# Gated linear attention in a fused decoder layer: two heads' queries side by side as one block-diagonal operand, dense keys and states

## The reference

```
log_a = log_sigmoid(a_lr @ w_a2 + b_a) / 16
bcum  = cumsum of log_a within a chunk
q_t, k_t = q / 8 * exp(bcum), k * exp(-bcum)
o_intra = where(tril, q_t @ k_t.T, 0) @ v
state   = exp(b_last) * state + (k * exp(b_last - bcum)).T @ v      # per head, 64 x 128
o_inter = q_t @ state before the chunk
o = rmsnorm(o_intra + o_inter) * silu(r)
```

## Time and profile before

| | |
|---|---|
| Median of 3 runs | 1683.11 us (1680.85 to 1890.51) |
| Profiled execution, its own time | 1687.72 us |
| Its span (slowest core) | 1686.6 us (cores: 1673.0 to 1686.6) |
| PE busy | 1628.0 us, 97%, 7859 matmuls |
| VectorE / ScalarE busy | 872.0 us / 730.4 us |
| Mean granted clock of TensorE | 0.992 of full speed on this core |
| DMA | 249.10 MB, mean 148 GB/s |

### The profile page before, as it was taken

The page is one execution under the profiler, slowest core; times in us unless marked ns, Lnnn a source line. Parts: engine busy times, 40 slices in busy tenths (PEclk is TensorE's granted clock), DMA queues, the critical chain, the costliest instruction groups (busy, mean ns, idle before and its releaser), DMA issues.

```text
span 1686.6 us, 24322 instructions; the slowest of 8 cores (1673.0 to 1686.6 us)
## 1 busy us (share of the span) xinstructions
PE 1628.0 (97%) x7859; PEld 753.9 (45%) x7859; DVE 872.0 (52%) x1490; ACT 730.4 (43%) x1182; POOL 120.6 (7%) x228
## 2 busy tenths in 40 slices
PE   6999999998999999999999999999999999999997
PEld 2445444434444444444444444454444444444443
DVE  6662442435765566654565644645645464433336
ACT  5213001046872256952477862268993221210114
POOL 0102011100000000000000000000000011001000
PEclk9999999999999999999999999999999999999999
DMA  9779999898566575555998774886464455623212
GB/s 212 106 114 124 139 125 110 129 148 208 104 146 157 151 154 111 111 130 167 252 207 181 159 192 151 256 220 154 133 192 129 159 157 157 178 70 100 76 38 100
DMA packets 80425, 249.10 MB, mean 148 GB/s; under 512 B 9440, under 2 KB 13808, under 8 KB 79856
## 3 DMA queue, kind: packets, MB, share of 16 engines
q0 software_dynamic: 28864, 107.49, 38.2%
q1 hardware_dynamic: 51440, 140.06, 26.9%
HBM read 282.91 MB, written 54.00 MB: 200 GB/s over the span
## 4 chain that ended last, share of the span: by engine, by line
PE 89%; DMA 4%; DVE 3%; ACT 3%; issue 2%; POOL 0%; DVEq 0%; ACTq 0%; SPq 0%; POOLq 0%
PE ps_all L562 88%; DMA ring<-f1g 2%; ACT mb L588 1%; DVE hS L600 1%; DMA ring<-wb 1%; ACT ma L588 1%; ACT L588 1%; DMA ring<-f2d 1%; DVE ntm L600 0%; DMA hS<-x 0%; DVE mb L595 0%; ACT fa L588 0%; DVE aF L595 0%; DVE gU L600 0%; ACT B L611 0%
## 5 line engine op out<-in xcount | busy, mean ns | idle before, releaser
L562 PE MATMUL ps_all<-ntm,ring 128*128 128x512 bf16 x2224 | 530.5, 381 | 5.1 <-ACT ma L588 2.2
L562 PE MATMUL ps_all<-B,ring 128*128 128x512 bf16 x2016 | 450.4, 379 | 2.8 <-DVE gU L600 1.0
L562 PEld LDWEIGHTS ps_all<-ntm,ring 128*128 128x128 bf16 x2224 | 216.3, 98 | 267.1 <-issue 21.1
L588 ACT ACTIVATE fa<-ps_all 128x512 f32<-128x512 f32 x170 | 101.4, 598 | 468.9 <-PE ps_all L562 460.5
L562 PEld LDWEIGHTS ps_all<-B,ring 128*128 128x128 bf16 x2016 | 195.9, 98 | 237.7 <-issue 8.3
L562 PE MATMUL ps_all<-aF,ring 128*128 128x512 bf16 (+1 forms) x1264 | 294.3, 375 | 3.7 <-DVE hS L600 1.7
L600 DVE SCALAR_TENSOR_TENSOR hS<-ps_all,hS 128x512 f32<-128x512 f32 (+1 forms) x256 | 170.0, 672 | 99.6 <-PE ps_all L562 98.4
L595 DVE TENSOR_TENSOR aF<-fa,ps_all 128x512 bf16<-128x512 f32 x148 | 101.3, 686 | 226.0 <-PE ps_all L562 219.6
L562 PEld LDWEIGHTS ps_all<-aF,ring 128*128 128x128 bf16 x1264 | 123.4, 98 | 147.5 <-issue 10.7
L588 ACT ACTIVATE mb<-ps_all 128x512 bf16<-128x512 f32 (+1 forms) x304 | 161.5, 576 | 39.0 <-PE ps_all L562 36.0
L588 ACT ACTIVATE ma<-ps_all,hv 128x512 f32<-128x512 f32 x104 | 71.2, 687 | 183.1 <-PE ps_all L562 162.2
(11 more groups left out here) (129 smaller groups left out, 1215.1 us busy)
## 6 DMA issues: line engine op xcount, KB each, us to landing
ring<-wb SPq DMA_DIRECT2D x112, 512.0 KB, 4.4
ring<-f1g POOLq DMA_DIRECT2D x44, 512.0 KB, 10.4
ring<-f2bg POOLq DMA_DIRECT2D x44, 512.0 KB, 3.6
wb<-wm POOLq DMA_DIRECT2D x28, 512.0 KB, 14.7
ma<-spill SPq DMA_DIRECT2D x48, 256.0 KB, 5.5
ring<-wb SPq DMA_DIRECT2D x48, 256.0 KB, 3.7
ring<-f2g POOLq DMA_DIRECT2D x22, 512.0 KB, 8.6
f2bg<-ring SPq DMA_DIRECT2D x22, 512.0 KB, 5.5
```

What stands on the lines that cost most here:

```text
L562: i = e.matmul(_ap(o), lhsT=_ap(l), rhs=_ap(r), start=st, stop=sp)
L588: f.add([("act", lambda e: e.activation(out=_ap(out), in_=_ap(in_), func=func, scale=_ap(scale), **kw), c_act(out, bias is not None))], ou ...
```

## The change

- q of a pair is written into `qz[pr]` (128 x 1024), block-diagonal: head 0's 64 rows in the columns 0 to 511, head 1's 64 rows in 512 to 1023, the rest zero. Two products on 64 rows in place of one on 128.
- k is used as it is. `ktz` and its copies are gone.
- The scores of a pair are one matmul of 256 columns with the moving operand [128, 2, 128] taken from qz.
- The state of a pair is dense, 128 rows (two heads' keys) by 128 value columns: `gU` and `gS` are 128x128. Block-diagonal q selects the head. `blk` and its load are gone. gU is updated in two pieces of 64 rows, from the two diagonal blocks of `pd`, and gS by a tensor_scalar.
- In the output, the carried product comes first, one matmul of 256 columns a pair, then v by am for each head, 128 columns.
- v's weights are cut in halves of K, all 512 columns: 8 matmuls of 512 columns for 128 tokens.
- k's working tile is kept until the last chunk; q needs none.

```
-    ktz = [T(f.sb(f"ktz{i}", [128, TT], BF16)[:], f"ktz{i}") for i in range(4)]
+    qz = [T(f.sb(f"qz{i}", [128, 2 * TT], BF16)[:], f"qz{i}") for i in range(2)]
-    gU = [T(f.sb(f"gU{i}", [128, 256], F32)[:], f"gU{i}") for i in range(2)]
+    gU = [T(f.sb(f"gU{i}", [128, 128], F32)[:], f"gU{i}") for i in range(2)]
...
-        f.dma("pool", blk, blk_d, nbytes=131072, after=f.last_pe)
...
 u_q:
-                stt(st["q"].bf()[:, pr * TT:(pr + 1) * TT], p, 0.125, st["E"][pr], ALU.mult, ALU.mult)
+                for o2 in range(2):
+                    rows = slice(64 * o2, 64 * o2 + 64)
+                    stt(qz[pr][rows, o2 * TT:(o2 + 1) * TT], p[rows, :], 0.125, st["E"][pr][rows, :], ALU.mult, ALU.mult)
 u_k:
-                for o2 in range(2):
-                    o = o2 * 64
-                    cp(ktz[pr * 2 + o2][o:o + 64, :], kb[o:o + 64, pr * TT:(pr + 1) * TT], eng="dve", rate=4.0)
 u_v:
-                st["wv"] = [mload("gv", i, 8) for i in range(2)]
+                st["wv"] = [mload("gv", i, 4) for i in range(2)]
...
-                mm([(p[:, v * 256:(v + 1) * 256], nM[k][:, i * 128:(i + 1) * 128], st["wv"][v][:, k, :], k == 0, k == 7)
-                    for v in range(2) for k in range(8)])
+                mm([(p, nM[k][:, i * 128:(i + 1) * 128], st["wv"][k // 4][:, k % 4, :], k == 0, k == 7) for k in range(8)])
 u_chunk:
-            q = [st["q"].bf()[:, pr * TT + i * 128:pr * TT + (i + 1) * 128] for pr in range(2)]
+            q = [qz[pr][:, :].re("p (h n) -> p h n", h=2)[:, :, csl] for pr in range(2)]
+            k = [st["k"].bf()[:, pr * TT + i * 128:pr * TT + (i + 1) * 128] for pr in range(2)]
...
-            mm([(pa[:, h4 * 128:(h4 + 1) * 128], ktz[h4][:, csl], q[h4 // 2], True, True) for h4 in range(4)])
+            mm([(pa[:, pr * 256:(pr + 1) * 256].re("p (h n) -> p h n", h=2), k[pr], q[pr], True, True) for pr in range(2)])
...
-            for h4 in range(4):
-                o = po[:, h4 * 128:(h4 + 1) * 128]
-                g.append((o, v[:, h4 * 128:(h4 + 1) * 128], am[:, h4 * 128:(h4 + 1) * 128], True, False))
-                g.append((o, gS[n % 2][h4 // 2][:, (h4 % 2) * 128:(h4 % 2 + 1) * 128], q[h4 // 2], False, True))
+            for pr in range(2):
+                g.append((po[:, pr * 256:(pr + 1) * 256].re("p (h n) -> p h n", h=2), gS[n % 2][pr], q[pr], True, False))
+                for h4 in (2 * pr, 2 * pr + 1):
+                    hsl = slice(h4 * 128, (h4 + 1) * 128)
+                    g.append((po[:, hsl], v[:, hsl], am[:, hsl], False, h4 % 2 == 1))
...
-                stt(gU[pr], gU[pr], gp, pd[:, pr * 256:(pr + 1) * 256], ALU.mult, ALU.add)
-                stt(gS[(n + 1) % 2][pr], gU[pr], gdec[par][pr][:, i:i + 1], blk, ALU.mult, ALU.mult)
+                for o2 in range(2):
+                    rows = slice(64 * o2, 64 * o2 + 64)
+                    stt(gU[pr][rows, :], gU[pr][rows, :], gp[rows, :],
+                        pd[rows, pr * 256 + o2 * 128:pr * 256 + (o2 + 1) * 128], ALU.mult, ALU.add)
+                ts(gS[(n + 1) % 2][pr], gU[pr], gdec[par][pr][:, i:i + 1], None, ALU.mult)
...
-    raw_at = [o_mla + [o_gla[:, i, :] for i in range(4)], o_x + ktz]
+    raw_at = [o_mla + [o_gla[:, i, :] for i in range(4)], o_x + [qz[i // 2][:, i % 2 * TT:(i % 2 + 1) * TT] for i in range(4)]]
```

More of the change, by code:

```diff
@@ L468, in build_program @@
     ident_d = din("ident", [128, 128])
-    blk_d = din("blk", [128, 256])
     smask_d = din("smask", [128, TT])
@@ L523, in build_program @@
     ident = T(f.sb("ident_s", [128, 128], BF16)[:], "ident")
-    blk = T(f.sb("blk_s", [128, 256], BF16)[:], "blk")
     smask = T(f.sb("smask_s", [128, TT], BF16)[:], "smask")
@@ L528, in build_program @@
     eps_c = T(f.sb("eps_c", [128, 1], F32)[:], "eps_c")
-    gU = [T(f.sb(f"gU{i}", [128, 256], F32)[:], f"gU{i}") for i in range(2)]
-    gS = [[T(f.sb(f"gS{j}_{i}", [128, 256], BF16)[:], f"gS{j}_{i}") for i in range(2)] for j in range(2)]
+    gU = [T(f.sb(f"gU{i}", [128, 128], F32)[:], f"gU{i}") for i in range(2)]
+    gS = [[T(f.sb(f"gS{j}_{i}", [128, 128], BF16)[:], f"gS{j}_{i}") for i in range(2)] for j in range(2)]
     gdec = [[T(f.sb(f"gd{j}_{i}", [128, 4], F32)[:], f"gd{j}_{i}") for i in range(2)] for j in range(2)]
@@ L678, in late_constants @@
             memset(gS[0][i], 0.0)
-        for i in range(4):
-            memset(ktz[i], 0.0)
+        for i in range(2):
+            memset(qz[i], 0.0)
         for kc in range(16):
@@ L984, in u_gates @@
                 st["Ei"].append(l)
-            st["q"], st["k"] = M2.get(), M2.get()
+            st["k"] = M2.get()
         def u_q():
@@ L1012, in u_kt @@
             cp(st["kt"].bf(), pb, rate=1.9)
-            M2.put(st["k"])
         def u_v(half):
             if half == 0:
-                st["wv"] = [mload("gv", i, 8) for i in range(2)]
+                st["wv"] = [mload("gv", i, 4) for i in range(2)]
                 st["v"] = [M2.get() for _ in range(2)]
@@ L1062, in u_chunk @@
             if i == 3:
-                M2.put(st["q"], st["kt"], *st["v"])
+                M2.put(st["k"], st["kt"], *st["v"])
         def u_x(hh):
@@ L1463, in _prep_shared @@
     for i in range(2):
-        block("gv", i, w_in[:, o[5] + i * 256:o[5] + (i + 1) * 256])
+        block("gv", i, w_in[i * 512:(i + 1) * 512, o[5]:o[6]])
         block("gr", i, w_in[:, o[7] + i * 256:o[7] + (i + 1) * 256])
@@ L1482, in _prep_shared @@
     f2g, f2d = ffn_w("ffn2_wg", "ffn2_wu", "ffn2_wd")
-    blk = np.zeros((128, 2, 128), f32)
-    blk[0:64, 0] = 1.0
-    blk[64:128, 1] = 1.0
     smask = np.ones((128, TT), f32)
@@ L1488, in _prep_shared @@
     return {
-        "vecs": vecs, "utri": (jj <= tq).astype(f32), "ident": (jj == tq).astype(f32), "blk": blk.reshape(128, 256),
+        "vecs": vecs, "utri": (jj <= tq).astype(f32), "ident": (jj == tq).astype(f32),
         "smask": smask, "wa2": np.ascontiguousarray(g("gla_w_a2")[0]),
```

## The result

After: 1692.02 us, median of 7 runs (1688.95 to 1976.87). Before, on the same chip: 1681.70 us, median of 7 (1680.25 to 1890.51). The ratio is **1.0056, 95% interval 1.0045 to 1.0067**: the change makes the kernel 0.56%, some 9 us, slower. The profiled execution of after took 1693.14 us. Ratios and means leave out executions in which one die ran at a lower clock.

The account below looks back on a forecast made before the run. PE bounds the kernel, its matmuls busy 1628.0 of 1686.6 us. PE −0.42 us, with 0 each for pieces, VectorE and planner, takes the median 1683.11 to 1682.7, given as 1682.5; range 1673 to 1694.

Parts of the forecast that it names:

- It hides behind PE: Mixer stretches: VectorE's net +0.2 us costs nothing, as PE is 95 to 98% busy and VectorE 54 to 79%.
- I take 0: Planner's new order in the mixer stretches: counted as 0, since no row favours a side; bounds −6.6 to +6.4 us.
- The sum before "It hides": VectorE's busy time: q +5.5, k copies −4.6, gU +6.7, gS −7.4, together +0.2 us on 872.
- if that cover were gone: VectorE's cost if PE did not hide it: 0.2 us by the sum, 16 us by the upper ends.
- The sentence on q: Before chunk 0: q's factors take 1.4 us more a tile, against 1.1 less in ktz copies chunk 0 also awaited.
- The planner's term: Idle time of the four mixer stretches under a shifted plan: 0 taken, between −6.6 and +6.4 us.
- a worse plan: Rival: new order costs +3 to +7 us, up to 1690, state product's bank held longer contributing; 15 in 100.
- PE's term: TensorE: 192 fewer matmuls, same columns, in v, scores and carried product; 0.42 us less, all on the path.
- The rival of pieces: Scores and carried product: a two-piece moving operand costs a second start, up to +6.6 us, 1689.7; 10 in 100.
- The rival of pacing loads: Chunks' small matmuls are paced by their weight loads, so fewer matmuls save 5.6 us: 1677.5; 3 in 100.
- v's blocks, the start: v's weights keep slots, loads and bytes; raw inputs at the start fit qz's halves with 3 us slack; no cost.
- blk's load: Start of the kernel: dropping this 128 KB load on POOL's queue taken as 0, at most −0.5 us.

Follow-up runs that it names:

- e13: After with its own plan kept to the last place, but q's product and gU's update each one whole VectorE instruction (parts of the result left out); ratio to before 1.0034.
- e9: The change's instructions in before's order, but q's product and the gU and gS updates as before (parts of the result left out); ratio to before 1.0000.
- e14: The change with the state product as two matmuls of 64 stationary columns a pair and one gU update, in before's order; ratio to before 1.0039.
- e3: Before with v's edit alone, planned anew; ratio to before 1.0116.
- e7: Before with v's edit alone, planned at its old cost so every order stays before's; ratio to before 0.9997.
- e12: The change with the state product in 64-stationary-column matmuls, one gU update a pair, and other planner constants; ratio to before 0.9950, 1672.59 us.

## Why the prediction was wrong, step by step

The forecast was 0.4 us less and 1682.5 us in all; 1692.02 was measured, and 0.56% or some 9 us more than before. That it lies inside the range, 1673 to 1694, is luck: its upper end left 7 us for operands in pieces, which cost nothing, or for mixers that idle more, which became better.

**Two steps failed: the one that put VectorE at zero, "It hides behind PE", and the planner's "I take 0".** By e13 the first is worth 0.22% or 3.7 us of after's loss, the second 0.34% or 5.7 us.

**VectorE.** The sum before "It hides" was off by 4.4 us: +0.2 forecast, 872.0 to 876.6 measured. Taking the parts on the old plan, where VectorE's busy time repeats to 0.3 us: q's halves +5.7 (forecast 5.5), copies −3.9 (−4.6), gU and gS +1.1 (−0.7; most of the difference is gS, 286 ns and not 250). In busy time on an engine that is idle for half of the span that is little, and it doesn't say why PE lost time. The error is that gains and costs were netted as if they lay at one place. The q halves put 1.4 us a tile in front of attention's masks, in a row of VectorE work without a gap; the copies were removed from where nobody waited (e9, without them, runs as before). And the shares of 54 to 79% busy that the step rested on are means over 74 to 150 us; the cover was asked for at 423 to 426 us, where VectorE was full already in before. What the prediction named as the price "if that cover were gone", 0.2 us by the sum, should have been the added instructions alone: 5.5 us of q and 6.7 of gU, as an upper bound. Measured on the cores' mean: 3.1, and 2.3 for gU and gS together.

The sentence on q ("its 1.4 us more a tile stand against 1.1 less in the ktz copies") asked who waits for q, and chunk 0 was the right answer. Who else is queued behind q on VectorE was not asked.

**The planner's term.** e13 leaves 0.34% of 1681.7, 5.7 us, to the plan. Its bounds (−6.6, +6.4) held by luck, as they were derived from the mixers' idle alone. With the plan alone (e13) that went down by 4.1 us, the stretches between rose by 4.8, and an estimated 2.7 us are the lower granted clock, a term that the prediction did not have. The mechanism was the rival "a worse plan" (15 in 100), with the wrong place. Its added condition, the state product's bank held longer, is seen in gU's waits, 1 us more, not in the plan.

**PE's term** was right as far as it can be seen: 7667 loads, v at 215.8 ns (forecast 216), scores at 108 (109). Its 0.42 us is too small for these runs; v alone measured 0.9997 on the old plan.

**The rival of pieces** is refuted by the two rows by form, 6.1 us for 32 matmuls either way, and by e9. **The rival of pacing loads** is refuted with it: e9, with 192 loads fewer, runs at 1.0000, where that rival asked for 0.9967. The Trainium skill's page "TensorE: Matmul & The Clock Gate" (section "Back-to-back issue gap") has about 131 ns a matmul for 512 columns in a real stream; the v product, with a load for each matmul, steps at 215.8, and the measurement decides.

**v's blocks, the start:** 0 was right; e9 contains both. For blk's load 0 is not contradicted, but e9 still has that load, and no run takes it away alone.

What stays open: why the planner, with its usual constants, does better for before's operations (1.0000) than for any neighbour of them; why e14 has two groups; and why some orders go with a lower clock than others.

## What to carry to other kernels

Cover is local: for each instruction that grows, read the other engine's timeline at that very place and ask what is queued behind it, and do not net it against work removed elsewhere. Where a list scheduler orders the program, an edit also draws a new order, and orders of the same instructions lay 0.9 to 1.2% apart here (1.2 between e3 and e7), more than any term of the edit. So measure the instructions on the old order, measure the order by itself (changed planned costs, same instructions), try several orders of each version before judging it, and look for the loss outside the stretches that were edited.

## What the runs showed of the hardware

In after, TensorE's clock fell to its lower level right behind 9 us in which PE was busy for 94%. The page's core at 883 us, the table by stretches, then PE's timeline:

```profile
874.00:883.00 9.00, 8.44 (x32) 2.75 (x30) 6.03 (x10) 6.17 (x11) 1.05 (x2) 0.95 1.00 254
883.00:888.00 5.00, 4.78 (x12) 1.74 (x13) 0.00 (x0) 2.26 (x4) 0.00 (x0) 0.50 0.64 111
```

```profile
881.49 1.57 PE L560 MATMUL ps_all<-cs 16*128 16x512 f32 x2
...
884.67 0.63 PE L560 MATMUL ps_all<-mb,B 128*128 128x512 bf16 x1
```

The granted clock is 0.50 for these 5 us, that is 1.2 GHz, and a 512-column matmul takes 630 ns instead of 379. What PE had done just before was two f32 matmuls of 16 rows, twice; that they are the reason is not shown, and core 4 ran the same order there at 1.00. In narrow stretches this fall reaches from about 882 to 889 us. Which core has one differs within a single execution. Core 6 has six such falls ahead of its last 40 us (near 94, 387, 397, 882, 1397 and 1647), 24 us in all, core 4 only two (near 92 and 392), 7 us. A matmul takes near to twice as long in them, so a fall costs up to half of its length: an estimated 12 us against 3.4. That is most of what lies between the two cores' spans, 1692.0 and 1682.1 us.

A VectorE product on 64 partitions takes as long as one on 128 (688 and 686 ns at 512 columns). Four matmuls with 64 stationary columns and 128 moving ones, into alternate halves of the rows, save nothing against two with 128 stationary and 256 moving ones: they take 0.30 us from the first start to the last end against 0.38, but with the later start before them the whole is 0.1 us longer (e12 and after, above).
